# Summing the partial products of nine conditioning pieces: four products of one column, or a fold and one product of four columns

## The reference

```
cond = silu(c)                                  # c: (1, 1024)
mod = (cond @ w_ada + b_ada)                    # w_ada: (1024, 9216) -> nine vectors of 1024
h = modulate(rms_norm(x, gain), mod[shift], mod[scale])
x = x + 0.5 * mod[gate] * ((silu(h @ w_gate) * (h @ w_up)) @ w_down)
```

## Time and profile before

| | us |
|---|---|
| Median of three runs | 1216.65 (1216.47 to 1219.16) |
| The profiled execution | 1214.66 |
| Its span | 1212.5 |
| PE busy | 1183.7 (98%) |
| DVE busy | 796.3 (66%) |
| ACT busy | 510.9 (42%) |
| POOL busy | 110.5 (9%) |
| Granted TensorE clock, mean | 0.996 |

### The profile page before, as it was taken

The page is one execution under the profiler, slowest core; times in us unless marked ns, Lnnn a source line. Parts: engine busy times, 40 slices in busy tenths (PEclk is TensorE's granted clock), DMA queues, the critical chain, the costliest instruction groups (busy, mean ns, idle before and its releaser), DMA issues.

```text
span 1212.5 us, 18972 instructions
## 1 busy us (share of the span) xinstructions
PE 1183.7 (98%) x7577; PEld 1055.5 (87%) x7577; DVE 796.3 (66%) x1071; ACT 510.9 (42%) x646; POOL 110.5 (9%) x166
## 2 busy tenths in 40 slices
PE   6999999999999999999999999999999999999997
PEld 5789999998889987868887788888889999998887
DVE  5788888766786567676563256665878888762232
ACT  6445544561213645455343322233535554552322
POOL 2000000002220123333020001100000000000000
PEclk9999999999999999999999999999999999999999
DMA  9423333337983121212211445633123333322211
GB/s 367 153 73 112 110 108 109 113 99 268 329 293 124 37 69 37 66 39 71 70 62 44 139 157 181 215 108 104 36 73 117 109 109 109 107 96 96 96 61 71
DMA packets 115130, 143.55 MB, mean 118 GB/s; under 512 B 4085, under 2 KB 102785, under 8 KB 115073
## 3 DMA queue, kind: packets, MB, share of 16 engines
q1 hardware_dynamic: 106800, 113.32, 28.2%
q0 software_dynamic: 8064, 29.36, 6.9%
q10 hardware_dynamic: 208, 0.08, 0.0%
HBM read 140.65 MB, written 2.10 MB: 118 GB/s over the span
## 4 chain that ended last, share of the span: by engine, by line
PE 87%; DVE 7%; ACT 4%; issue 1%; POOL 1%; DVEq 0%; ACTq 0%; POOLq 0%
PE PS L794 28%; PE PS L550 16%; PE PS L552 15%; PE PS L551 15%; PE PS L873 4%; PE PS L913 1%; PE PS L595 1%; PE PS L597 1%; PE PS L596 1%; PE PS L708 1%; DVE ACC L1725 1%; ACT WH L1107 1%; PE PS L900 1%; PE PS L883 1%; DVE ACC0b L1736 1%
## 5 line engine op out<-in xcount | busy, mean ns | idle before, releaser
L1623 DVE TENSOR_TENSOR WL<-RAW,WH 128x2048 fp32r<-128x2048 f32 (+2 forms) x55 | 120.6, 2194 | 131.8 <-ACT WH L1107 131.7
L550 PE MATMUL PS<-HH,WH 128*128 128x512 f32 (+2 forms) x488 | 186.4, 382 | 4.3 <-DVE HL L1651 2.9
L1107 ACT ACTIVATE WH<-RAW 128x2048 fp32r<-128x2048 f32 (+2 forms) x55 | 100.6, 1829 | 199.5 <-PE PS L552 193.0
L552 PE MATMUL PS<-HH,WL 128*128 128x512 f32 (+2 forms) x488 | 178.9, 367 | 0.0
L551 PE MATMUL PS<-HL,WH 128*128 128x512 f32 (+2 forms) x488 | 178.8, 366 | 0.0
L794 PE MATMUL PS<-HH,WH 128*128 128x256 f32 x576 | 162.5, 282 | 0.4 <-DVE WL L1910 0.4
L794 PE MATMUL PS<-HL,WH 128*128 128x256 f32 x576 | 162.1, 281 | 0.0
L794 PE MATMUL PS<-HH,WL 128*128 128x256 f32 x576 | 162.1, 281 | 0.0
L550 PE MATMUL PS<-UH,WH 128*128 128x512 f32 (+1 forms) x416 | 148.2, 356 | 0.0
L552 PE MATMUL PS<-UH,WL 128*128 128x512 f32 (+1 forms) x416 | 147.3, 354 | 0.0
L551 PE MATMUL PS<-UL,WH 128*128 128x512 f32 (+1 forms) x416 | 147.2, 354 | 0.0
(11 more groups left out here) (304 smaller groups left out, 2308.4 us busy)
## 6 DMA issues: line engine op xcount, KB each, us to landing
RAW<-in_ffn_w_in_dram SPq DMA_DIRECT2D x42, 1024.0 KB, 5.1
ADAW<-in_w_ada_dram POOLq DMA_DIRECT2D x56, 512.0 KB, 5.4
RAW<-in_w_in_mix_dram SPq DMA_DIRECT2D x22, 1024.0 KB, 5.2
RAW<-in_ffn_w_down_dram SPq DMA_DIRECT2D x16, 1024.0 KB, 5.0
ADA<-in_w_ada_dram SPq DMA_DIRECT2D x16, 512.0 KB, 10.0
RAW<-in_ffn_w_down_dram SPq DMA_DIRECT2D x7, 768.0 KB, 4.3
RAW<-in_w_out_dram SPq DMA_DIRECT2D x3, 1024.0 KB, 5.0
XST<-in_x_dram SPq DMA_DIRECT2D x4, 512.0 KB, 5.1
```

Source lines behind the costliest of these rows:

```text
L550: mm(ps, whi, ahi, start=start, stop=False)
L552: return mm(ps, wlo, ahi, start=False, stop=stop)
L1107: A(WH[slot(n)][:, 0:size], RAW[slot(n)][:, 0:size], ACT.Copy).then_inc(unit_hi, 1)
L1623: V.tensor_tensor(WL[s][:, 0:size], RAW[s][:, 0:size], WH[s][:, 0:size].bitcast(F32), ALU.subtract)\
```

## The change

For pieces 4 to 12 the sum over the partitions is made in three steps. Four transfers within SBUF, issued by POOL, take each 128 columns of the accumulator (128 partitions) to 32 partitions of FOLD_IN, where four rows of the source lie side by side. POOL adds the halves of FOLD_IN (128 x 256), then the two quarters left (128 x 128), into FOLD. PE makes one product with FOLD as the weight and GSEL, a table of four columns, as what passes: column g has ones in partitions 32g to 32g + 31. GSEL is made at the start by five memsets of POOL.

With it come: two accumulators in turn, so that the terms of a piece wait for the fold transfers of the piece two before and no longer for a product; the product at k-step 6 instead of 4 (k-step 5 in units of six); POOL's loads one piece ahead of the fold in its queue; the bias of a piece one unit later in DVE's order, ahead of the additions and the split. Pieces 13 to 17 keep the four products.

```diff
+            def fold_rows(piece):
+                pool.wait_ge(ada_acc, DB * (piece + 1))
+                if piece > 4:
+                    pool.wait_ge(folded, piece + 1)
+                for g in range(4):
+                    pool.dma_start(FOLD_IN[32 * g:32 * g + 32, :, :].rearrange("r q m -> r (q m)"),
+                                   ACC[piece % 2][:, g * P:(g + 1) * P]).then_inc(fold_in, 16)
+                pool.wait_ge(fold_in, 64 * (piece - 3))
+                nc.gpsimd.tensor_tensor(FOLD_IN[:, 0:2, :], FOLD_IN[:, 0:2, :], FOLD_IN[:, 2:4, :], ALU.add).then_inc(half_fold, 1)
+                pool.wait_ge(half_fold, piece - 3)
+                if piece > 4:
+                    pool.wait_ge(ada_red, piece)
+                nc.gpsimd.tensor_tensor(FOLD[:, :], FOLD_IN[:, 0, :], FOLD_IN[:, 1, :], ALU.add).then_inc(folded, 1)
+
+            load_ada(4)
             for piece in range(4, LATE_PIECE):
-                load_ada(piece)
+                if piece + 1 < LATE_PIECE:
+                    load_ada(piece + 1)
+                fold_rows(piece)
...
             def ada_reduce(piece):
-                pe.wait_ge(ada_acc, DB * (piece + 1))
                 pe.wait_ge(mod_ready, piece)
+                if piece < LATE_PIECE:
+                    pe.wait_ge(folded, 5 + piece - 3)
+                    mm(PS[:, 6, 0:4], FOLD[:, :], GSEL[:, :], start=True, stop=True).then_inc(ada_red, 1)
+                    return
+                pe.wait_ge(ada_acc, DB * (piece + 1))
                 for m in range(4):
-                    ins = mm(PS[:, 6, m:m + 1], ACC[:, m * P:(m + 1) * P], ONES[:, 0:1], start=True, stop=True)
+                    ins = mm(PS[:, 6, m:m + 1], ACC[0][:, m * P:(m + 1) * P], ONES[:, 0:1], start=True, stop=True)
...
-                    reducing = ada_reduce_at(4, piece0 + piece) if piece0 is not None and piece0 + piece >= 4 else None
+                    reducing = ada_reduce_at(6 if piece < 2 else 5, piece0 + piece) if piece0 is not None and piece0 + piece >= 4 else None
...
-                    if k == 4:
+                    if k == 6:
                         ada_reduce(LATE_PIECE - 2 + piece)
...
             def ada_piece(piece):
-                dve.wait_ge(ada_red, piece)
+                if piece >= LATE_PIECE:
+                    dve.wait_ge(ada_red, piece)
+                elif piece > 5:
+                    dve.wait_ge(fold_in, 64 * (piece - 5))
...
+                        ahead = 4 + 6 * i + 3 * q + piece if ada else 0
+                        if ahead > 5:
+                            add_ada_bias(ahead - 2)
```

More of the change, by code:

```diff
@@ L105, in trunk_program @@
         GKW = sb("GKW", [RANK, 256])
+        GSEL = sb("GSEL", [P, 4])
         H_BYTES = DB * T * 4
@@ L142, in trunk_program @@
         YF = [place(f"YF{s}", [P, T], 94208 + 2048 * s) for s in range(2)]
-        ACC = place("ACC", [P, AW], 102400)
+        ACC = [place("ACC0", [P, AW], 102400), place("ACC1", [P, AW], HO + H_BYTES + 8192)]
+        FOLD_IN = place("FOLD_IN", [P, 4, P], HO)
+        FOLD = place("FOLD", [P, P], HO + 2048)
         ADA0 = place("ADA0", [P, 2, DB, 2, AW], 0)
         XST = place("XST", [P, TT, D], 65536)
-        ACC0 = [place("ACC0a", [P, 2 * AW], NT), place("ACC0b", [P, 2 * AW], 2 * FB * T * 4)]
+        ACC_FIRST = [place("ACC_FIRSTa", [P, 2 * AW], NT), place("ACC_FIRSTb", [P, 2 * AW], 2 * FB * T * 4)]
         TN0 = place("TN0", [P, DB, T], HO + H_BYTES)
@@ L205, in trunk_program @@
         ada_red = sem("ada_red")
+        fold_in, half_fold, folded = sem("fold_in"), sem("half_fold"), sem("folded")
         mod_ready = sem("mod_ready")
@@ L473, in _ @@
             done(nc.gpsimd.memset(RST[:, :], 1.0))
+            nc.gpsimd.memset(GSEL[:, :], 0.0).then_inc(folded, 1)
             pool.wait_ge(consts, cn[0])
+            for g in range(4):
+                pool.wait_ge(folded, g + 1)
+                nc.gpsimd.memset(GSEL[32 * g:32 * g + 32, g:g + 1], 1.0).then_inc(folded, 1)
+            pool.wait_ge(folded, 5)
             done(nc.gpsimd.affine_select(out=IDENT[:, :], in_=IDENT[:, :], compare_op=ALU.not_equal, fill=1.0,
@@ L678, in ada0_reduce @@
                     whole = not PE_TERMS[half]
-                    ins = mm(PS[:, 6, col:col + 1], ACC0[half][:, AW * s + m * P:AW * s + (m + 1) * P],
+                    ins = mm(PS[:, 6, col:col + 1], ACC_FIRST[half][:, AW * s + m * P:AW * s + (m + 1) * P],
                              ONES[:, 0:1], start=whole, stop=whole or (s, m) == (1, 3))
@@ L1732, in ada0_term @@
                 if k == 0:
-                    V.tensor_scalar(ACC0[half][:, :], w, COND[:, 0:1], None, ALU.mult).then_inc(ada_acc, 2 + 2 * skipped)
+                    V.tensor_scalar(ACC_FIRST[half][:, :], w, COND[:, 0:1], None, ALU.mult).then_inc(ada_acc, 2 + 2 * skipped)
                 else:
                     dve.wait_ge(ada_acc, before)
-                    V.scalar_tensor_tensor(ACC0[half][:, :], w, COND[:, k:k + 1], ACC0[half][:, :], ALU.mult, ALU.add)\
+                    V.scalar_tensor_tensor(ACC_FIRST[half][:, :], w, COND[:, k:k + 1], ACC_FIRST[half][:, :], ALU.mult, ALU.add)\
                         .then_inc(ada_acc, 2)
@@ L1816, in ada_piece @@
                         dve.wait_ge(ada_in[j], 16 * (piece - 3))
-                    ada_term(k, ACC[:, :], ada_buffer(piece, j)[:, k % 2, :], DB * piece + k)
+                    ada_term(k, ACC[piece % 2 if piece < LATE_PIECE else 0][:, :], ada_buffer(piece, j)[:, k % 2, :], DB * piece + k)
             def add_ada_bias(piece):
@@ L2020, in down @@
                         n = base_n + 3 * q + piece
+                        ahead = 4 + 6 * i + 3 * q + piece if ada else 0
+                        if ahead > 5:
+                            add_ada_bias(ahead - 2)
+                            if ahead < 8:
+                                cs = slice(4 * ahead - 24, 4 * ahead - 20)
+                                dve.wait_ge(mod_ready, ahead - 1)
+                                self_wait(V.tensor_scalar(GATE[:, 0, cs], MOD[:, 2 * DB:3 * DB][:, cs], 0.5, None, ALU.mult))
                         if piece == 2:
@@ L2034, in down @@
                         if ada:
[L2035 to L2041, removed]
                             ada_piece(ahead)
@@ L2045, in _ @@
                 down(N_F1DOWN, i, 0, 8, 10, 0, ada=True, qs=(0, 1) if i == 0 else (0,))
+            add_ada_bias(LATE_PIECE - 2)
             last_split_lo(0)
```

2 lines of the change are left out of this document (1 added, 1 removed).

## The result

The changed kernel takes 1238.7 us (median of 4 runs, 1235.0 to 1243.9) against 1217.4 us of the kernel before (4 runs, 1216.5 to 1219.2): a ratio of 1.0176, 95% interval 1.0131 to 1.0222. The forecast was 1222.5, its range ended at 1231. The direction was right, the size was not: +21 us in place of +5.9.

What follows compares the result with a forecast made beforehand. PE, busy 98% of the span, was taken as the bound; 11.5 us of new waits less 5.4 and 0.2 saved gave +5.9, so 1222.5 us from the runs' median of 1216.65, range 1213.5 to 1231.

Steps and rivals of the forecast that it cites:

- The product's saving: PE, pieces 4 to 12: two passes instead of eight gain 5.4 us, no DVE wait for products 0.4: 5.8 us.
- The additions: POOL's two fold additions per piece: 0.8 us for 128x256 and 0.5 for 128x128, plus 0.2 us of semaphores.
- The mechanism: Down stage of FFN 1: fold later than the product's place, so in-order PE waits; POOL's loop exceeds PE's 10.6 us units.
- The sum: Whole change: 11.5 us of waits less 5.4 and 0.2 gives +5.9 us.
- the waits: PE idle before the new products of pieces 4 to 12: 11.5 us together, first in piece 4 with about 3 us.
- the 11.7 of the forecast: Middle of the stage: one fold every 11.7 us, set by POOL's four loads, four folds and two additions in order.
- What I costed at nothing: Starting memsets (some 0.8 us, covered), bias moved ahead of the split in DVE's loop, FOLD's reuse: no cost.
- the landing: Fold transfers on POOL's queue: 3.0 us from issue, not before the preceding load's 5.4 us landing plus 0.3.
- Fold ready: e + 6.0: All four fold transfers landed 6.0 us after e, the end of a piece's last term on DVE.
- that exception: First four loads, issued together from 270.87: reached DVE after 4.6 us, then 2.16 us more for each.
- The third rival: POOL's queue slower than taken: loads land 1.8 us apart, 12.6 us a piece, +12.2, 1228.9 us; chance 0.24.
- the break-even case: Rival: landing, loads and additions at their low ends give +0.5 us, or -2.0 with short issues; 1214.6 to 1219, chance 0.28.

Runs made afterwards that it cites:

- hold of 7: Changed kernel, product waits kept, each fold's transfers and additions replaced by a POOL hold of the forecast's length (11 memsets): 1226.5 us, ratio 1.0077.
- two accumulators: Changed kernel without any fold, keeping the four one-column products with the change's other edits (later places, DVE's new order): 1219.3 us, ratio 0.9999 to before.
- the two holds: Changed kernel with transfers and additions replaced by POOL holds: forecast's length (11 memsets) 1226.5 us, trace's length (16 memsets) 1242.1 us.
- Fold beside: Changed kernel with the fold running but unused, PE making the four old products straight from the accumulators: 1237.6 us, ratio 1.0151 to before.
- filled waits: Changed kernel with 67 idle matmuls ahead of PE's waits for the fold in six pieces: 1243.3 us, ratio 1.0205 to before.
- Late additions: Changed kernel with POOL making each piece's additions after three of the next piece's loads, products one unit later, pieces 4 and 12 unfolded: 1221.4 us, ratio 1.0030.
- no fold: Changed kernel without fold transfers and additions; the four-column product reads a constant tile and waits only for the terms: 1215.2 us, ratio 0.9972 to before.
- transfers only: Changed kernel with 36 fold transfers issued, no additions, no landing wait ahead of the loads, product by a constant: 1219.0 us, ratio 1.0002 to before.
- the hold without a wait: Kernel without fold work (product of a constant), POOL held about 9.9 us by 17 memsets before the next loads, pieces 4 to 11: 1227.3 us, ratio 1.0084.

## Why the prediction was wrong

**Right.** The product's saving, nearly (5.8 forecast, 6.3 in the stage; the new product costs 0.22 us, not 0.3). The additions: 0.73 and 0.51 us in the middle, by the line's records, 0.8 and 0.5 forecast. The mechanism: a fold too slow for the distance, a PE that waits in order, a POOL loop longer than a piece. The hold of 7 puts the forecast's fold on the chip: stage +4.7 for +5.9. The sum agrees better than its parts, and that much is luck: the waits were 7.7 us for 11.5, and the cycle of 11.6 us was not POOL's loop, as the 11.7 of the forecast was. What I costed at nothing cost nothing (two accumulators: ratio 0.9999).

**The step that failed** is the landing: "I take 3.0 us from the start of the issue, and not before the load in front of it on the same queue has landed, which I set at 5.4 us, the page's median, plus 0.3." A fold took 6.0 us in the middle, counted from its own issue. The row of the loads in the changed kernel (270 to 400 us), and that of the one load at 295.64, the last of four issued together:

```profile
DMA to landing us min/median/max: 4.3/6.2/8.5
...
L514 POOL DMA_DIRECT2D ADAW<-in_w_ada_dram x1: 732/732/732, 295.6 to 295.6; - x1
DMA to landing us min/median/max: 8.1/8.1/8.1
```

The eight loads that stood right in front of a fold landed after 6.1 to 8.1 us, 7.2 in the mean, where I had 5.4, and the last of the four fold transfers 0.7 to 2.9 us behind that load, 1.4 in the mean, where I had 0.3. The two longest of these, 2.9 and 2.7, stand beside a 1 MB load of SP issued within 0.3 us of one of the fold's transfers, which the sum had nowhere. From the issue of the load to the fold's end the forecast had 5.9 us; it was 7.0 to 9.3, 8.6 in the mean. The loads ahead had been issued at least 1.6 us apart before except the first four, at 270.87; the changed loop sends all four in 2.9 us in four of eight pieces, and the fold behind them. So "Fold ready: e + 6.0" became, over the nine pieces, e + 4.1 (the last, no load ahead) to e + 13.3, 9.6 in the mean, the waiting of POOL for the fold before included. The rows of that exception had the number, loads 2.16 us apart at DVE, and I used 1.5; issued together, they now landed 1.7 to 2.0 us apart.

The Trainium skill ("DMA: Bandwidth & Descriptors", section "Anatomy of one DMA — SWDGE (gpsimd) path") gives 2.15 us for 64 KB, an estimate from its fixed cost and rate. The trace agrees where no load is in flight (2.1 to 2.3 us for the changed kernel's last fold) and not behind the loads (6.0 in the middle), and there the measurement decides.

**Where +5.9 became +23 in the stage.** By the two holds: 4.7 us with the forecast's length and 23.1 with the trace's. The difference of 18.4 us is the landing's error, 3 us a piece times eight pieces and less what other waits swallow. The third rival, loads 1.8 us apart, a POOL loop of 12.6 us a piece and 1228.9 us, named the right place with the right consequence; the loop was 13.7. The range had a slip of its own: it starts at 1213.5 as the low end of the break-even case, which the list of rivals gives as 1214.6.

**What I had not seen.** I priced the fold at the product's wait alone. Fold beside shows that the wait is only where the loss appears: take it away, and the loads, the terms, the bias and the splits are late instead, for 18.2 of the 23.0 us in the stage. The next piece's loads, which are queued behind POOL's wait, were in the forecast's table, but had no price of their own. The granted clock (0.50 to 0.70 over 4 us after the long waits) had no term either; filled waits say that in this stage it was covered by POOL's loop.

**Open.** Outside the stage something remains: kernels whose stage is level with before or shorter are slower than it tells. Late additions have +0.7 us in the stage and +3.7 in the time, no fold -6.3 and -3.4, transfers only -4.3 and +0.2, hold of 7 +4.7 and +9.4 (times by the ratios); two accumulators, without the new product, show nothing of it, and the hold without a wait, which has the new product, shows nothing clear of noise (+9.2 and +10.2). A low granted clock in the mixer behind the stage looks like a cause: the trace of no fold has 0.83 from 510 to 520 and from 540 to 550 us, where the trace before has 1.00. But two accumulators, as fast as before, have the same (us, PE busy, PEclk, DMA share, GB/s):

```profile
510.00:520.00 10.00, 10.00 (x63) 0.83 0.33 107
540.00:550.00 10.00, 8.81 (x48) 0.83 0.00 0
```

So these stretches don't tell the kernels apart, and no run shows where the 3 to 5 us outside the stage come from.

## What to carry to other kernels

Where an in-order queue waits for a landing, price what stands behind the wait first: here the next loads, whose delay alone cost 18 of the 23 us when nobody waited for the fold. A transfer's landing is to be read from rows with the same loads ahead of it, not from the page's median. And a wait that is wanted goes into a gap the queue already has: the same additions, one piece later, took the stage from 158.6 to 136.3 us (with the product a unit later and two of nine pieces left unfolded, which without the new order had 150.8).

## What the runs showed of the hardware

A 64 KB transfer within SBUF landed in 2.1 us at the least; 2.3 in the middle with two of the four 512 KB loads issued behind it instead of ahead; 6.0 behind all four, and 5.8 from another engine's queue: the queue made no difference. Four 512 KB loads issued within 2.9 us landed 1.7 to 2.0 us apart, the last after 7.9 to 8.1 us. POOL issued a 64 KB transfer in 0.55 us, against 0.72 for 512 KB. After PE had stood for 4.8 us the granted clock was 0.53 over the next whole stretch of 4 us, and matmuls started 0.43 us apart in place of 0.23. POOL's second addition took 0.45 or 0.78 us, but 2.38 in two of nine pieces of fold beside.
